# How far ahead of the matmuls the weights are split: the look-ahead constants 5 and 4 become 6 and 6, and the calls inside the MLP loop move

## The reference

```
def _mlp(x, norm_g, w1, w2):
    h = _rmsnorm(x, norm_g)
    return jnp.square(jax.nn.relu(h @ w1)) @ w2
```

## Time and profile before

| what | value |
|---|---|
| median of 3 runs | 980.49 us (979.64 to 981.13) |
| the profiled execution | 979.64 us, its span 977.8 us, mean granted TensorE clock 0.995 |
| TensorE busy | 961.5 us, 98% of the span |
| VectorE, ScalarE, GpSimd busy | 766.8, 606.7 and 130.0 us (78%, 62%, 13%) |
| chain that ended last | TensorE 92%, VectorE 5% |
| low parts of weights (line 1648) | 312 instructions, 364.3 us, mean 1196 ns |
| high parts of weights (line 1111) | 312 instructions, 310.0 us, mean 1024 ns |
| HBM | 178 GB/s over the span |

### The profile page before, as it was taken

The page is one execution under the profiler, slowest core; times in us unless marked ns, Lnnn a source line. Parts: engine busy times, 40 slices in busy tenths (PEclk is TensorE's granted clock), DMA queues, the critical chain, the costliest instruction groups (busy, mean ns, idle before and its releaser), DMA issues.

```text
span 977.8 us, 15188 instructions
## 1 busy us (share of the span) xinstructions
PE 961.5 (98%) x5810; PEld 847.1 (87%) x5810; DVE 766.8 (78%) x1157; ACT 606.7 (62%) x1003; POOL 130.0 (13%) x173
## 2 busy tenths in 40 slices
PE   9999989999999999999998999999999999999997
PEld 8878879999998888888887999999888888988885
DVE  6888687999975767786657889885758989878884
ACT  6688665777765554455455766664535867766662
POOL 2731023022001102220002000000550110000000
PEclk9999999999999999999999999999999999999999
DMA  9984544647572663345455456564444463633631
GB/s 338 307 225 184 174 155 147 226 134 244 187 244 87 215 214 131 129 133 212 173 172 172 173 189 234 180 234 166 151 155 168 138 207 99 204 130 129 215 129 44
DMA packets 110342, 174.80 MB, mean 179 GB/s; under 512 B 4288, under 2 KB 73024, under 8 KB 110272
## 3 DMA queue, kind: packets, MB, share of 16 engines
q1 hardware_dynamic: 109840, 173.40, 52.6%
q10 hardware_dynamic: 432, 0.44, 0.1%
HBM read 172.78 MB, written 1.05 MB: 178 GB/s over the span
## 4 chain that ended last, share of the span: by engine, by line
PE 92%; DVE 5%; issue 1%; ACT 1%; POOL 0%; POOLq 0%; DVEq 0%
PE ps L472 19%; PE ps L473 19%; PE ps L474 19%; PE ps L579 11%; PE ps L532 8%; PE ps L530 5%; DVE wlo L1648 2%; PE ps L548 2%; PE ps L743 1%; PE ps L723 1%; PE ps L529 1%; PE ps L546 1%; PE ps L711 1%; PE ps L667 1%; DVE arena L1775 1%
## 5 line engine op out<-in xcount | busy, mean ns | idle before, releaser
L1648 DVE TENSOR_TENSOR wlo<-raw,whi 128x1024 fp32r<-128x1024 f32 (+1 forms) x312 | 364.3, 1196 | 26.9 <-ACT whi L1111 26.6
L1111 ACT ACTIVATE whi<-raw 128x1024 fp32r<-128x1024 f32 (+1 forms) x312 | 310.0, 1024 | 47.4 <-PE ps L474 30.2
L472 PE MATMUL ps<-hT,whi 128*128 128x256 f32 x584 | 165.9, 284 | 0.0
L474 PE MATMUL ps<-hT,wlo 128*128 128x256 f32 x584 | 165.4, 283 | 0.0
L473 PE MATMUL ps<-hT,whi 128*128 128x256 f32 x584 | 165.4, 283 | 0.0
L472 PE MATMUL ps<-whi,hT 128*128 128x512 f32 (+1 forms) x312 | 122.1, 391 | 0.0
L474 PE MATMUL ps<-whi,hT 128*128 128x512 f32 (+1 forms) x312 | 120.1, 385 | 0.0
L473 PE MATMUL ps<-wlo,hT 128*128 128x512 f32 (+1 forms) x312 | 120.0, 385 | 0.0
L532 PE MATMUL ps<-hT,whi 128*128 128x512 f32 x336 | 119.7, 396 | 0.0
L472 PEld LDWEIGHTS ps<-hT,whi 128*128 128x128 f32 x584 | 111.7, 191 | 1.7 <-issue 0.3
L473 PEld LDWEIGHTS ps<-hT,whi 128*128 128x128 f32 x584 | 111.7, 191 | 1.3
(11 more groups left out here) (253 smaller groups left out, 1632.8 us busy)
## 6 DMA issues: line engine op xcount, KB each, us to landing
raw<-in_w SPq DMA_DIRECT2D x64, 1024.0 KB, 5.4
raw<-in_w_in SPq DMA_DIRECT2D x34, 1024.0 KB, 4.9
raw<-in_w_in_o SPq DMA_DIRECT2D x24, 1024.0 KB, 5.1
raw<-in_w_out_o SPq DMA_DIRECT2D x8, 1024.0 KB, 4.9
raw<-in_w_in_e SPq DMA_DIRECT2D x5, 1024.0 KB, 13.0
raw<-in_w_mem SPq DMA_DIRECT2D x4, 1024.0 KB, 10.1
raw<-in_w_out_e SPq DMA_DIRECT2D x4, 1024.0 KB, 4.8
raw<-in_w_out SPq DMA_DIRECT2D x4, 1024.0 KB, 4.9
```

What stands on the lines that cost most here:

```text
L472: e.matmul(o, a[0], b[0], start=start, stop=False)
L474: return e.matmul(o, a[1], b[0], start=False, stop=stop)
L1111: e.activation(split_half(i)[0], raw_half(i), ACT.Copy).then_inc(*up("hi", ("hi", i)))
L1648: e.tensor_tensor(l, raw_half(i), h.bitcast(F32), ALU.subtract).then_inc(*up("lo", ("lo", i)))
```

## The change

The two constants become 6 and 6, so that every `used(...)` outside of the tables reaches one half further on ScalarE and two on VectorE. In the MLP loop `second` goes. With i as the first half of w2 tile j - 1, ScalarE now makes parts up to i + 4 ahead of relu and square, parts up to i + 7 ahead of u_high, and up to the tile's last half + 5 behind u_high (i + 8 for a tile of four halves, nothing new for one of two). VectorE makes parts up to i + 4, then to i + 6, then u_sums, then up to the tile's last half + 5, then u_low. For j = 0 the first call alone is left, which reaches w1 tile 0's second half + 5. For j = 16 the calls with i as the last w2 tile stay.

```diff
--- before.py
+++ after.py
@@ -27,7 +27,7 @@
 NCONST = 1920
 
 NRAW, NHI, NLO = 4, 7, 7
-HI_AHEAD, LO_AHEAD = 5, 4
+HI_AHEAD, LO_AHEAD = 6, 6
 HI_ROW = (6, 7, 8, 8, 11, 12, 13, 14, 15, 16, 17, 18, 19, 20, 21, 22, 23, 24, 25, 26)
 LO_ROW = (5, 6, 7, 8, 8, 11, 12, 13, 14, 15, 16, 17, 18, 19, 20, 21, 22, 23, 24, 25)
 ARENA = 19456
@@ -356,10 +356,6 @@
         def ur1(p):
 
             return tuple(t[:, 0:4, :].rearrange("p (k b) n -> p k (b n)", b=2) for t in us[p % 2])
-
-        def second(layer, j):
-
-            return first_half["w2", layer, j - 1] if j else first_half["w1", layer, 1]
 
         def slots(p):
 
@@ -1357,14 +1353,16 @@
                 x_high(stage, gcol)
                 row_squares(stage, x3, av(0, 2048, 2), [at("x", before, 1), at("x", before, 3)])
                 for j in range(17):
-                    i = second(layer, j)
                     if j < 16:
-                        weights_to(i + 6)
+                        used(("w1", layer, j), 1)
                         relu_squared(layer, j)
-                        weights_to(i + 7)
+                    if j >= 1:
+                        i = first_half["w2", layer, j - 1]
+                        weights_to(i + 2 + HI_AHEAD)
+                    if j < 16:
                         u_high(layer, j)
-                    else:
-                        used(("w2", layer, 15), 1)
+                    if j >= 1:
+                        weights_to(last_half[tile_of[i]] + HI_AHEAD)
                     if layer == 0:
                         decays(j)
 
@@ -2082,15 +2080,19 @@
                 stage = f"mlp{layer}"
                 row_reciprocals(stage)
                 for j in range(17):
-                    i = second(layer, j)
                     if j < 16:
-                        weights_to(i + 5)
-                        if j < PLAIN:
-                            u_sums(layer, j)
-                        weights_to(i + 7)
+                        used(("w1", layer, j), 1)
+                    if j >= 1:
+                        i = first_half["w2", layer, j - 1]
+                        weights_to(i + 1 + LO_AHEAD)
+                    if j < PLAIN:
+                        u_sums(layer, j)
+                    if j >= 1:
+                        weights_to(last_half[tile_of[i]] + LO_AHEAD)
+                    if j < 16:
                         u_low(layer, j)
-                    else:
-                        used(("w2", layer, 15), 1)
+                    if j >= 1:
+                        used(("w2", layer, j - 1), last_half[tile_of[i]] - i)
                     if PLAIN <= j < PLAIN + 3:
                         sums_shared(stage, j - PLAIN)
                     if layer == 0 and j == 1:
```

## The result

The changed kernel takes 1006.4 us (median of 4 runs, 1005.45 to 1007.08) against 980.16 us (979.64 to 981.13) of the kernel before on the same chip: a ratio of 1.026, 95% interval 1.0248 to 1.0272. Slower was forecast, but by 6.5 us; it is 26. The profiled execution has a span of 1003.8 us, against 977.8.

A forecast was written before the change was run, and what follows sets the result against it. TensorE was taken as the bound, 98% busy. Terms -6.3 - 3.4 + 10.4 + 3.3 + 0.8 + 1.7 = +6.5 us gave 987.0 us as median; forecast range 983 to 991, overall 974 to 992.

The forecast's parts named there:

- What bounds the kernel: TensorE, busy 98% of the span; two waits of 4.1 us for u's low part are most of its short waits.
- The first waits: Start of both MLPs: TensorE's wait for u_low falls from 4.15 to 1.0 us, -6.3 us for two.
- the clock: Behind the MLPs' first waits: no fall to half clock after the shorter wait, -3.4 us for two.
- The seven-product steps: MLP steps with four-half tiles: u_sums, u_high, high part, low part, u_low form an uncovered chain; +10.4 us.
- The ends: End of each MLP: x_high queues behind a high part waiting for its buffer; +3.3 us in all.
- The start: Program start: ScalarE waits for the next transfer first, VectorE's norm scales come later; +0.8 us, between 0 and 2.3.
- The other stages: Outside the MLPs only the constants act; losses in three places: start +0.8, MoBA +1.2, cross attention +0.5 us.
- MoBA: Block attention: VectorE's split waits for the same step's high part, delaying rope blocks; +1.2 us, between 0 and 2.1.
- cross attention: Same pattern as MoBA once, with less at stake; +0.5 us, 0 to 1.5.
- D: Rival: clock swings in each of a dozen new short gaps, 20 us on top, 1007 us; chance 0.03.
- signs of being wrong: No waits in w2 tiles 3, 7, 11, or granted clock 0.50 anywhere behind a short gap.
- Rival A: Faster: seven-product steps absorb the chain; 976.6 us, or 973 if the MLPs' ends hide too; chance 0.18.

The follow-up runs named there:

- c1_start: Kernel before, only the first step of each MLP changed: two fewer parts per engine ahead of relu, square, u_high, sums and u_low; 968.19 us.
- a4_tail: Changed kernel, the tile's last low part on VectorE made behind u_low instead of ahead of it; 996.79 us.
- d3_hihead: a3_lag1 with ScalarE making the tile's last high part ahead of u_high in the MLP loop; 982.88 us.
- f4_after65: Changed kernel with look-aheads 6 and 5 instead of 6 and 6, in the MLPs too; 972.27 us.
- f2_end: d3_hihead with the look-aheads of the kernel before at j = 16, on ScalarE and VectorE; 980.38 us.
- g1_65end: f4_after65 with the reach of the kernel before at j = 16; 969.17 us.
- a3_lag1: Changed kernel with look-aheads 6 and 5 outside the MLPs, 6 and 6 kept in the MLP loop; 989.77 us.
- a1_const66: Kernel before with only the two look-aheads set to 6 and 6, old MLP loop kept; 990.65 us.
- b1_55: Kernel before with look-aheads 5 and 5, old MLP loop; 994.3 us.
- b2_65: Kernel before with look-aheads 6 and 5, old MLP loop; 977.28 us.
- d2_xorder: a1_const66 with VectorE's reciprocal of the softmax sums ahead of the low part in cross attention; 988.84 us.
- f1_xboth: d2_xorder with ScalarE's high part also ahead of the exponentials in cross attention; 983.91 us.
- d1_both: a3_lag1 and a4_tail's edit together in the changed kernel; 981.66 us.
- e1_c65: c1_start with look-aheads 6 and 5 in place of 5 and 4; 967.96 us.
- g2_after54: Changed kernel with look-aheads 5 and 4 of the kernel before, leaving only the new MLP loop order; 971.04 us.
- a2_loop54: Changed kernel with look-aheads 5 and 4 outside the MLPs, 6 and 6 in the new MLP loop; 995.19 us.

## Why the prediction was right or wrong

**What bounds the kernel: right.** TensorE, with two repairable waits.

**The first waits, -6.3, and the clock, -3.4: right** (-9.0 for -9.7); c1_start shows that the place was worth 11.8. The remaining wait was forecast as 1.0 us and is 1.19, with clock 1.00 behind it.

**The seven-product steps, +10.4: right in mechanism, 3.5 too small.** a4_tail and d3_hihead each cut the chain and each removes the waits at tiles 3, 7 and 11. MLP 1 lost 4.4 for 3.7. In MLP 0 the two waits at tiles 7 and 8 came as said (2.23 and 0.62 us), and the clock fell behind the first (1.7). Two waits ahead of them, 0.23 us at tile 6 and 0.67 us before the w1 product that uses low part 76, weren't foreseen; together they cost 1.4. The part of the decay rows on ScalarE and of GpSimd in this wasn't tried. What I missed is that the chain hangs on one number: with LO_AHEAD at 5, f4_after65 has the same calls and no chain.

**The ends, +3.3: right** (+3.7; 2.3 and 1.4 for 2.0 and 1.3), and f2_end and g1_65end remove 3.1 of it.

**The start, +0.8: too small**, 1.9. TensorE waits 1.1 us for a key norm scale (L1701) behind a split. That was named, but sized nearer to the wrong end. The wait is gone where VectorE stays one part behind (a3_lag1).

**"The other stages", MoBA +1.2 and cross attention +0.5: this is the step that failed.** It holds 13.8 of the 19.5 us of the error. The text had it that "before, VectorE ran one high part behind ScalarE; with both at 6 it needs the one of the same step". That was the cause, and I priced it by one place only. In MoBA the first rope block's wait is 1.20 us, as worked out for it; behind it a second of 1.66 was not looked at, nor the clock (1.5: the stage lost 4.8 here and 3.3 in a1_const66, with the same two waits and no fall). For cross attention I wrote "the same pattern once, with less at stake", without a row. There the pattern isn't one delay but a chain to and fro between the two engines: maximum, exponentials, high part, low part, reciprocal and gate, in each of four steps, with 2.0 to 2.6 us of idle time on VectorE in three of them (2.58 at 894.82 and 903.75) and about 2 on ScalarE. b1_55 loses the same 13.9 us in the two stages at 5 and 5, a3_lag1 and b2_65 nothing. d2_xorder takes the reciprocal out of the chain and leaves the 4.1 us; f1_xboth takes out the high part's place behind the exponentials too, and they fall to 0.7. The longest wait thus hangs on the way from the maximum over the exponentials, the high part and the low part to the gate, not on the reciprocal. That the chain also closes to a loop, in which each step delays the next, isn't shown.

**The rivals.** D gave the right time (1007) by luck, for the wrong reason. It had a dozen short gaps swing the clock; the clock fell three times, for 2.9 us more than before, and of the ten waits for u_low only one, the longest (2.23 us), was followed by a fall. The Trainium skill's "TensorE: Matmul & The Clock Gate", section "A second HAM failure mode: psum-queue depth-cycling", on repeated micro-idles, is not borne out at such gaps, seven of which came in the MLPs with the clock at 1.00 behind them (1.2 to 1.3 us each). One of the prediction's own signs of being wrong did come, half clock behind a short gap: at 784.97 us, behind a wait of 1.20 us and in one of 1.66. Rival A fell for this kernel, but came near the time of f4_after65. The Trainium skill's "Perfetto Trace Analysis", section "Identifying Performance Opportunities", says that the same gap repeating on the engine that should be busy can mean that there isn't enough memory on the chip for the next tile. Here it didn't: all kernels have the same 4 raw buffers and 7 and 7 for the parts, and the recurring waits went when less work stood in front of the urgent instruction (a4_tail, f4_after65).

## What to carry to other kernels

When two engines make one thing in two stages, the difference of their look-aheads is a parameter of its own, and here it mattered more than either: keep the consumer one part behind the producer, or the two programs, each in order, wait for each other within a step. Before changing such a number, go through every stage that uses it and ask what stands ahead of the producer's instruction and behind the consumer's, and whether work on one feeds work on the other; then follow the chain through the step by its rows, and do it in each stage, for a delay of one instruction doesn't price it (1.7 us forecast, 15.5 measured). The view that shows it is the consumer's idle time before the group (26.6 to 85.6 us here), even where TensorE's waits are still few.

## What the runs showed of the hardware

Over 19 traces (all but d1_both's), each wait of TensorE of 3.5 us or more (12 of them, up to 4.15) had a fall of the granted clock to 0.50 (1.2 GHz) in it or within 1.5 us behind it. Of 19 waits between 2.0 and 3.3 us 9 had one, and the same wait in two kernels could go either way (2.46 us at 145 us: no fall in a1_const66, a fall in f1_xboth). Of waits up to 1.7 us none had, save a pair of 1.21 and 1.66 within 2 us, in 3 kernels of 6. A fall lasted 3.41 or 6.83 us, so it costs at most 1.7 or 3.4 us, less where TensorE is idle in it, and the second length wasn't in the trace before. The spread of the times goes with it, though no run shows it to be the cause: the kernels without a wait over 1.5 us (c1_start, e1_c65, f4_after65, g1_65end, g2_after54) agree within 0.1 to 0.7 us over four runs, most of those with waits of 2 to 4 us scatter by 2 to 5 (a2_loop54 by 0.5 only, the kernel before by 1.5, the changed one by 1.6). What decides between fall and none at 2 to 3 us stays open.
